# Experts one by one in blocks of 32 rows, instead of two by two in rounds of 64 each

## What is computed

```python
def moe(tokens, w_router, b_router, w1, w3, w2):
    scores = jax.nn.sigmoid(tokens @ w_router)
    # best group of 8 experts, then the two best experts in it
    _, e_idx = lax.top_k(jnp.where(in_group, sel, -jnp.inf), TOP_K)
    gate = jnp.take_along_axis(scores, e_idx, axis=-1); gate = gate / jnp.sum(gate, axis=-1, keepdims=True)
    # rows are grouped by expert; for the rows xb of expert e:
    y = (jax.nn.silu(xb @ w1[e]) * (xb @ w3[e])) @ w2[e]
    # a token's output is the sum of its two rows of y, each times its gate
```

## Time and profile before

| | us |
|---|---|
| median of 3 runs | 3428.88 (3427.94 to 3429.7) |
| the profiled execution | 3428.47 |
| its span, first to last instruction | 3426.3 |
| granted TensorE clock, mean | 0.949 |

### The profile page before, as it was taken

How to read it: one execution, slowest core, us unless ns; L and a number is a source line. 1 busy time by engine, 2 the same in 40 slices (tenths; PEclk the granted TensorE clock), 3 DMA queues, 4 the chain that set the end, 5 groups by cost and what they waited for, 6 DMA issues and landing times. The chain is left out here.

```text
span 3426.3 us, 48079 instructions
## 1 busy us (share of the span) xinstructions
PE 3128.9 (91%) x17203; PEld 1776.6 (52%) x17203; DVE 1422.9 (42%) x4218; ACT 835.0 (24%) x1611; POOL 260.7 (8%) x324
## 2 busy tenths in 40 slices
PE   6999976899999699999996999899999969999983
PEld 3666645645555444444443455477775534444441
DVE  2333346665474411111113688666665431111113
ACT  1111113466511000000002344355551100000001
POOL 0000004400060000000000000000002000000001
PEclk8999988899999699999998999999999979999996
DMA  9700075200052779999964222100003187899998
GB/s 345 297 25 24 13 292 165 80 1 1 1 167 80 272 292 392 411 411 411 381 239 171 80 86 74 68 1 1 1 1 131 68 332 283 326 411 411 411 410 328
DMA packets 217637, 676.22 MB, mean 197 GB/s; under 512 B 24004, under 2 KB 36468, under 8 KB 217460
## 3 DMA queue, kind: packets, MB, share of 16 engines
q1 hardware_dynamic: 188212, 564.31, 42.8%
q0 software_dynamic: 20176, 76.55, 6.0%
q10 hardware_dynamic: 9072, 33.03, 2.4%
HBM read 579.32 MB, written 94.50 MB: 197 GB/s over the span
## 5 line engine op out<-in xcount | busy, mean ns | idle before, releaser
L2678 PE MATMUL ps_u<-w_ring,work 128*64 128x256 f32 x3392 | 381.3, 382 | 11.1 <-DMA w_ring<-in_w 11.1
L2666 PE MATMUL ps_g<-w_ring,work 128*64 128x512 f32 x1696 | 377.2, 596 | 5.8 <-DMA w_ring<-in_w 5.8
L2697 PE MATMUL ps_y<-w_ring,work 128*64 128x512 f32 x1696 | 375.6, 595 | 0.0
L2678 PEld LDWEIGHTS ps_u<-w_ring,work 128*64 128x64 f32 x3392 | 244.5, 138 | 161.9 <-issue 32.9
L1705 PE MATMUL of_ps_r<-of_w,cat 128*128 128x512 f32 (+1 forms) x608 | 257.7, 580 | 3.0 <-ACT cat L1788 3.0
L2666 PEld LDWEIGHTS ps_g<-w_ring,work 128*64 128x64 f32 x1696 | 121.8, 138 | 251.5 <-issue 240.2
L423 PE MATMUL ps_r<-w,hT 128*128 128x512 f32 (+1 forms) x640 | 249.4, 546 | 1.5 <-ACT hT L482 1.5
L2697 PEld LDWEIGHTS ps_y<-w_ring,work 128*64 128x64 f32 x1696 | 117.1, 137 | 220.6 <-issue 220.6
L2752 DVE SCALAR_TENSOR_TENSOR work<-work,ps_g 128x512 f32<-128x512 f32 x53 | 36.4, 687 | 366.1 <-ACT work L2730 366.1
L1432 PE MATMUL mo_ps_o<-mo_w,mo_cT 128*128 128x512 f32 x416 | 186.1, 599 | 1.4 <-DMA mo_w<-in_e_w_out 0.9
L1705 PEld LDWEIGHTS of_ps_r<-of_w,cat 128*128 128x128 f32 x608 | 115.7, 194 | 127.1 <-issue 123.4
(11 more groups left out here) (511 smaller groups left out, 4334.6 us busy)
## 6 DMA issues: line engine op xcount, KB each, us to landing
w_ring<-in_w SPq DMA_DIRECT2D x768, 512.0 KB, 15.1
y_dram<-zeros POOLq DMA_DIRECT2D x2, 14080.0 KB, 65.8
y_dram<-work ACTq DMA_DIRECT2D x53, 512.0 KB, 6.7
ml_staging<-in_w_ada SPq DMA_DIRECT2D x9, 2048.0 KB, 11.9
w_ring<-in_w_ada SPq DMA_DIRECT2D x6, 2048.0 KB, 13.3
ml_spare<-in_w_ada SPq DMA_DIRECT2D x5, 2048.0 KB, 13.4
ml_arena<-ml_rows SPq DMA_DIRECT2D x40, 256.0 KB, 4.4
f_dram<-mo_f SPq DMA_DIRECT2D x18, 512.0 KB, 2.8
```

The costliest lines, as they stand in the source:

```text
L2666: mm = pe.matmul(ps_g[rows, :], xT[:, k, rows], weight(k // 2)[:, h, (k % 2) * DE:(k % 2 + 1) * DE], start=k == 0, stop=k == KD - 1)
L2678: mm = pe.matmul(ps_u[rows, f, 0:256], xT[:, k, rows], weight(4 + k // 2)[:, h, at:at + 256], start=k == 0, stop=k == KD - 1)
L2697: mm = pe.matmul(ps_y[rows, half, :], hT[:, k, rows], weight(8 + k)[:, h, half * 512:(half + 1) * 512], start=k == 0, stop=k == 3)
```

## The change

Experts go one by one, in blocks of 32 rows; an expert has at least two blocks. By the counts above there are 98 blocks in layer 0 and 89 in layer 1, in the order 2 6 2 6 2 4 2 4 2 4 2 4 2 4 2 4 2 4 2 3 2 3 and ten times 3, and 2 7 2 6 2 6 2 4 2 4 2 4 2 4 2 3 2 3 2 3 2 3 and ten times 2. The pool's gather reads 128 quarter rows of 1 KB, four blocks ahead; quarter q of the 32 tokens lies in partitions 32q to 32q+31. VectorE turns that in 32x32 blocks, and weights are loaded in the order of features that this gives (in pieces of 4 KB, as before). For each step of contraction the four column groups each make a quarter of the outputs: 128 columns of w1 and 128 of w3 in one matmul of 256, then 256 of w2. ScalarE brings the four quarters of y to whole rows with four copies of 32x256. PE puts the up part of a block ahead of the down part of the block before it. In `route` the order of experts is computed in fewer steps, `low` is 32 wide instead of 128, `high` has 149 columns (LISTW) for each of its parts instead of 56, and y_dram has 36 blocks of 128 rows instead of 55.

```diff
-NPAIR = NE // 2
-MAXB = 2 * T // HALF + NPAIR - 1
-LISTW = MAXB + 1
+UNIT = 32
+MAXB = 2 * T // UNIT + 2 * NE - 3
+AHEAD = 4
+LISTW = MAXB + 2 * AHEAD
+YB = -(-(MAXB + AHEAD - 1) * UNIT // P)
...
@@ route, tensor
         for a in range(2 * nt):
-            if a % PIECE == 0:
-                pe.wait_ge(low_in, a // PIECE + 1)
-            mm = pe.matmul(ps_l[:, 0:LISTW], low[:, a * P:(a + 1) * P], high[:, a * LISTW:(a + 1) * LISTW], start=a == 0, stop=a == 2 * nt - 1)
+            for q in range(P // UNIT):
+                mm = pe.matmul(ps_l[q * UNIT:(q + 1) * UNIT, 0:LISTW], low[:, a, :], high[:, a * LISTW:(a + 1) * LISTW], start=a == 0, stop=a == 2 * nt - 1)
...
@@ load_chunk
+        if c < 4:
+            src = A[("w1", "w3")[h]][layer, bass.ds(e, 1), :, :].rearrange("o (q c r k) n -> c q r (o k n)", q=P // UNIT, c=4, k=2)[c]
         else:
+            src = A["w2"][layer, bass.ds(e, 1), :, :].rearrange("o (q c r) n -> c q r (o n)", q=P // UNIT, r=UNIT)[2 * (c - 4) + h]
...
@@ experts, gpsimd
+        with pool.Fori(0, fours) as i:
+            for at in range(AHEAD):
+                pool.wait_ge(gathered[at], i * 16 + 16)
+                pool.wait_ge(x_turned, i * AHEAD + (at + 1))
+                pool.sem_inc(xs_free, 1)
+                pool.tensor_copy(xs, xg[:, at * 256:(at + 1) * 256]).then_inc(x_ready, 1)
+                pool.wait_ge(x_ready, i * AHEAD + (at + 1))
+                gather(nc.s_assert_within(i * AHEAD + (AHEAD + at), AHEAD, LISTW - 1, skip_runtime_bounds_check_because="rounds more than there are, which nothing reads"), at)
...
@@ experts, tensor
+        def up(u, gb):
+            pe.wait_ge(x_turned, gb + 2)
+            pe.wait_ge(h_ready, gb + 1)
+            for c in range(4):
+                take(u, c)
+                w = R.w[:, (u * CHUNKS + c) % RING, :, :]
+                for kk in range(2):
+                    for n in range(QU):
+                        rows = slice(n * UNIT, (n + 1) * UNIT)
+                        at = kk * DE + n * P
+                        mm = pe.matmul(ps_h[rows, :], xT[:, (2 * c + kk) * UNIT:(2 * c + kk + 1) * UNIT], w[:, :, at:at + P], start=c == 0 and kk == 0, stop=c == 3 and kk == 1)
+                        if kk == 0 and n == 0:
+                            mm.then_inc(w_used, 1)
+            mm.then_inc(up_done, 1)
+        def down(u, now):
+            pe.wait_ge(y_out, now)
+            pe.wait_ge(h_turned, now)
+            for i in range(2):
+                take(u, 4 + i)
+                w = R.w[:, (u * CHUNKS + 4 + i) % RING, :, :]
+                for kk in range(2):
+                    k = 2 * i + kk
+                    for n in range(QU):
+                        mm = pe.matmul(ps_y[n * UNIT:(n + 1) * UNIT, :], hT[:, k * UNIT:(k + 1) * UNIT], w[:, kk, n * 256:(n + 1) * 256], start=k == 0, stop=k == 3)
+                        if kk == 0 and n == 0:
+                            mm.then_inc(w_used, 1)
+            mm.then_inc(y_done, 1)
...
+        for u in range(NE):
+            start, more = span_of(pe, u)
+            if u:
+                up(u, start)
+                down(u - 1, start)
+            with pe.Fori(0, more) as b:
+                gb = inside(start + b + 1, 1, MAXB - 1)
+                up(u, gb)
+                down(u, gb)
...
+        for reached in (x_turned, up_done, y_done):
+            pe.sem_inc(reached, AHEAD)
@@ experts, scalar
+        def store(now, b, uses):
+            act.wait_ge(y_done, now)
+            act.wait_ge(y_st[b], uses * 16 + 16)
+            for n in range(QU):
+                w = act.copy(y[b * UNIT:(b + 1) * UNIT, n * 256:(n + 1) * 256], ps_y[n * UNIT:(n + 1) * UNIT, :])
+            w.then_inc(y_out, 1)
+            act.wait_ge(y_out, now + 1)
+            act.dma_start(R.y_dram[bass.ds(now * UNIT + -UNIT, UNIT), :], y[b * UNIT:(b + 1) * UNIT, :]).then_inc(y_st[b], 16)
...
@@ experts, vector
+        def hidden(gb):
+            dve.wait_ge(th_done, gb + 1)
+            dve.scalar_tensor_tensor(out=hr, in0=th, scalar=1.0, in1=ps_h[:, 0:P], op0=ALU.add, op1=ALU.mult).then_inc(th_used, 1)
+            dve.wait_ge(th_used, gb + 2)
+            dve.scalar_tensor_tensor(out=hr, in0=hr, scalar=0.5, in1=ps_h[:, P:2 * P], op0=ALU.mult, op1=ALU.mult).then_inc(h_ready, 1)
+        def turn_x(gb):
+            dve.wait_ge(x_ready, gb + 1)
+            dve.transpose(xT.rearrange("p (c k t) -> p c k t", c=4, k=2), xs.rearrange("p (c r k) -> p c k r", c=4, k=2)).then_inc(x_turned, 1)
+        def turn_h(gb):
+            dve.wait_ge(h_ready, gb + 2)
+            dve.transpose(hT, hr).then_inc(h_turned, 1)
...
+        with dve.Fori(1, total) as gb:
+            dve.wait_ge(up_done, gb + 1)
+            turn_x(gb + 1)
+            dve.wait_ge(h_turned, gb)
+            hidden(gb)
+            dve.wait_ge(y_done, gb)
+            turn_h(gb)
```

More of the change, by code:

```diff
@@ L2404, in _ @@
         own()
[L2405 removed]
+        dve.tensor_scalar(E_, rk, -2.0, float(2 * NE - 2), ALU.mult, ALU.add).then_inc(*c.up())
+        dve.tensor_scalar(at, rk, 2.0, 1.0, ALU.mult, ALU.add).then_inc(*c.up())
         own()
[L2407 to L2422, removed]
+        dve.tensor_tensor(at, at, E_, ALU.min).then_inc(*c.up())
         own()
@@ new lines, in experts, with inside, span_of @@
+    up_done, th_done, th_used, h_ready, h_turned = s("up_done"), s("th_done"), s("th_used"), s("h_ready"), s("h_turned")
+    y_done, y_out = s("y_done"), s("y_out")
+    y_st = [s(f"y_st{b}") for b in range(AHEAD)]
+    def total_rounds(eng):
+        return eng.value_load(R.table[0:1, NE:NE + 1], min_val=2 * NE, max_val=MAXB)
+    def inside(v, low, high):
+        return nc.s_assert_within(v, low, high, skip_runtime_bounds_check_because="MAXB rounds at most, two at least for an expert")
+    def span_of(eng, u):
+        entry = eng.value_load(R.table[0:1, u:u + 1], min_val=1, max_val=64 * 256 - 1)
+        return inside(entry // 64, 0, MAXB - 2 * NE) + 2 * u, inside(entry % 64, 1, T // UNIT)
@@ L2579, in _ @@
     @block.sync
     def _(sp):
-        def last_round(pair):
-            entry = sp.value_load(R.table[0:1, pair:pair + 1], min_val=0, max_val=32 * 64 - 1)
-            last = entry // 32 + entry % 32 + pair
-            return nc.s_assert_within(last, 0, MAXB - 1, skip_runtime_bounds_check_because="MAXB rounds at most")
-        for pair in range(1, NPAIR):
-            e = experts_of(sp, R, pair)
-            for c in range(PER_PAIR):
-                q = pair * PER_PAIR + c
+        for u in range(3, NE):
+            e = expert_of(sp, R, u)
+            for c in range(CHUNKS):
+                q = u * CHUNKS + c
@@ L2706, in _ @@
         pe.wait_ge(R.ada_done, 1)
         pe.wait_ge(R.tabled, 1)
-        for pair in range(NPAIR):
-            entry = pe.value_load(R.table[0:1, pair:pair + 1], min_val=0, max_val=32 * 64 - 1)
-            start = nc.s_assert_within(entry // 32, 0, MAXB - NPAIR, skip_runtime_bounds_check_because="MAXB rounds at most, one each for the pairs") + pair
-            rounds = nc.s_assert_within(entry % 32 + 1, 1, 32, skip_runtime_bounds_check_because="each pair has a round")
-            with pe.Fori(0, rounds) as b:
-                round_of(pair, nc.s_assert_within(start + b, 0, MAXB - 1, skip_runtime_bounds_check_because="MAXB rounds at most"))
+        up(0, 0)
```

312 lines of the change are left out of this document (107 added, 205 removed).

## The result

The changed kernel takes 6205.57 us (median of 4 runs, 6204.9 to 6209.05) against 3428.41 (3424.18 to 3429.7): a ratio of 1.811, 95% interval 1.8075 to 1.8138. Forecast was 3331 us.

The account below looks back on a forecast made before the run. The prediction took TensorE to bound the kernel, with weight transfers bounding late layer 1. From 3428.5 us it took 82 for layer 0 and 26 for layer 1 and added 10 around them: 3331 us, range 3295 to 3600.

Parts of the forecast that it names:

- the layers' sums: Expert stages: layer 0 from PE's blocks, 575 us against 656.9; layer 1 from DMA at 411 GB/s, 584 against 610.4.
- the weights' GB/s well below 360: Expert weight transfers: a rate listed as a sign that the forecast is wrong, pointing to rival 3.
- rival 3: Gathers: 1 KB pieces cost as much as 4 KB, both layers bound by DMA, 3490 us; chance 0.05.
- the 5 us added for 1 KB pieces: Layer 1 gathers: smaller pieces add 0.06 us a block, 5 in all.
- A block: Expert products on PE: 24 sets at 0.219 us, 5.26, plus 0.2 for PE's queue, gives 5.46 us.
- Rivals 1 and 2: TensorE: instruction stream bounds, change loses above 28 ns each, chance 0.28; or weight loads don't hide, 3820 us, chance 0.03.
- The chain: Between blocks, end of up to `hidden`: tanh, turning, two VectorE operations take 1.47 us, covered by a down of 1.75.
- Rival 4: Between blocks: the chain is longer than a down; block 5.8 to 6.3 us, total 3365 to 3430; chance 0.12.
- Changing expert: PE's sequencer between experts: 0.3 us open per expert, 9 us a layer, ends 0 and 1.1 each.
- Layer 0: First expert stage: 29 + 98 x 5.46 + 9 + 2 = 575 us against 656.9, so -82.
- Layer 1: Second expert stage, bound by DMA: 224.6 MB at 411 GB/s, 547 us, with additions 584 against 610.4, so -26.
- Around them: Outside the expert stages: table and list steps, larger `high`, extra blocks at the end; in sum +10 us.

Follow-up runs that it names:

- e1: Changed kernel with the weights' four row groups filled from interleaved rows (128 partitions outermost, one stride), x and h turned to match; 3323.15 us, 0.970 of the kernel before.
- e7: e1 with the second weight transfer of each chunk left out after the ring's first filling, so outputs are wrong; 3198.53 us.
- e10: e7 with the changed kernel's cheaper turning in place of e1's, outputs wrong; 3183.3 us.
- e4: Changed kernel with weight sources split in 8 groups of 16 rows instead of 4 of 32, outputs wrong; 4308.6 us.
- e8: Changed kernel with weight sources split in 16 groups of 8 rows instead of 4 of 32, outputs wrong; 3625.8 us.
- e2: Changed kernel with each weight transfer issued as four, one per group of 32 partitions, same addresses and bytes; 3960.39 us.
- e5: e1 with each weight transfer issued as four of 128 KB, one per group of 32 neighbouring partitions; 3928.76 us.
- e6: e1 with each weight transfer issued as four of 128 KB, each over every fourth partition; 4349.24 us.

## Why the prediction was wrong

The step that failed is in the layers' sums: "Weights are 201.3 MB ... 224.6 MB at 411 GB/s are 547 us", and for layer 0 the silent assumption that the same transfers stay under PE. The ground for it was the change's description, pieces "of 4 KB, as before". Pieces, bytes and issues did stay; the number of engines that carry a transfer did not, and no row of before showed it, as all its weight transfers had 128 partitions outermost. The term was priced by the nearest row and had no bound on its other side. With 4 engines it is 201.3 MB at 103 GB/s, a quarter of 411: 1954 us a layer; the stages took 2023 and 2018. That it is this step is shown by e1, which gives the transfers their engines back and comes to 3323.

The forecast named "the weights' GB/s well below 360" as a sign of being wrong, and tied it to rival 3. That rival does not hold: in e1 the stage moves 408 GB/s with all its 1 KB gathers in it, and by the packet records a gather leaves 32 packets of 4 KB at 166 ns there, where one of 4 KB rows left 128 at 163. So the 5 us added for 1 KB pieces were not there either.

Point by point, by e1, e7, e10 and the changed kernel's trace (stages of runs end here at the start of their last w2 matmul, 0.4 us before its end):
- **A block** at 5.46: 5.18 (e7). That is 0.216 a set with all between them, so the 24 sets of 0.219 were right and the 0.2 for PE's queue was not there. Rivals 1 and 2 are refuted.
- **The chain** at 1.47, read as the forecast did, from the end of up's slot: 1503.89 - 1502.42 = 1.47 us in e10, whose turning is the changed kernel's, and 1.50 in e7. The terms differ and make up for each other, which is luck: tanh starts 0.44 later (forecast 0.22), the two operations take 249 and 288 ns in the changed kernel (forecast 344 each), its turning 446 (forecast 425). It is covered, as up starts at 1504.15. Rival 4 is refuted.
- **ScalarE's copies** at 0.37: 363 ns. **POOL's copy** at 0.86: 399 ns. **The gather** at 0.98: 0.97.
- **Changing expert** at 9 us a layer: in e7, 543.5 less 98 x 5.18 less the start of 29 leaves 7 us, the wait of the first block's chain included, where the forecast had 9 + 2.
- **Layer 0** at 575: 580.7 in e1. Two errors that cancel, so that it comes close is luck: PE needs only 543.5 (e7), but 227 MB at 408 GB/s need 556, so DMA bounds layer 0 too. The two were compared only for layer 1.
- **Layer 1** at 584: 577.9 in e1, bound by DMA as forecast (with DMA out of the way, in e7, it is 489.8).
- **Around them** +10: the changed kernel has 6209.05 - 4040 = 2169 us outside the stages, before 3428.47 - 1267.3 = 2161: +8; e1 has 2165, +4.

In e1 it sums to 3428.5 - 76 - 32.5 + 4 = 3324: with the engines back, the forecast of 3331 is good to 8 us, in part by the luck named above.

## What to carry to other kernels

When a change rewrites the source pattern of a transfer, read its outermost dimension before its bytes and pieces: a few groups outermost left most DMA engines out here, and the symptom was a low DMA share beside waits for DMA. The packets of the queue told it at once: their number per transfer fell by one for each engine that was missing. Look for an index order that makes the partitions one stride, and put the permutation into the on-chip turning; here that, with the new order of reads, cost 1.5 us of 581 in layer 0.

## What the runs showed of the hardware

- Outermost dimension and DMA share: 4, 0.31; 8, 0.56; 16 and 128, 1.03 (the changed kernel, e4, e8, e1). 4 KB packets under way at a time: 3.9, 7.7, 14.5 and 14.3.
- With 16 engines at work, rows of DRAM read in other groups moved the rate from 408 to 341 GB/s, in e8's first 240 us to 273; a 4 KB packet took 194 ns instead of 160 (e1, e8, 1400 to 1600 us).
- Splitting 512 KB transfers in four over 32 partitions took it to 265 to 273 GB/s at a full share (e2, e5), over every fourth partition to 208 at a share of 0.68 (e6).
- TensorE held 192 instructions (96 loads of 32 columns on all rows, 96 matmul records of 256 columns) in 5.18 us, 27 ns each, block after block (e7).
- VectorE's turning of 128x256 f32 takes 446 ns reading every second number (the changed kernel) and 656 reading every eighth (e1); of 128x128, 312 one after another and 420 at every fourth.
